# Hybrid decoder step: the S5 half turn's transfers issued by GpSimd instead of ScalarE

## What is computed

```
bb_t = coef * (B u_t)                    complex
h_t  = a * h_(t-1) + bb_t                a = exp((lam_re + i lam_im) dt)
y_t  = Re-part of C h_t + d * u_t
```

## Time and profile before

| | |
|---|---|
| median of 3 runs | 1402.5 us (1401.43 to 1403.63) |
| the profiled execution | 1399.56 us |
| its span (first to last instruction) | 1397.8 us |
| PE busy | 1322.9 us (95%), granted clock 0.979 on average |
| DVE busy | 760.2 us (54%) |
| ACT busy | 449.5 us (32%) |
| POOL busy | 397.3 us (28%) |

### The profile page before, as it was taken

How to read it: one execution, slowest core, us unless ns; L and a number is a source line. 1 busy time by engine, 2 the same in 40 slices (tenths; PEclk the granted TensorE clock), 3 DMA queues, 4 the chain that set the end, 5 groups by cost and what they waited for, 6 DMA issues and landing times.

```text
span 1397.8 us, 32218 instructions
## 1 busy us (share of the span) xinstructions
PE 1322.9 (95%) x14024; PEld 1208.2 (86%) x14024; DVE 760.2 (54%) x1499; ACT 449.5 (32%) x809; POOL 397.3 (28%) x403
## 2 busy tenths in 40 slices
PE   5999999997999999999999999999999989899997
PEld 5898999987888988989898989988897589798885
DVE  7595744625444637173554637274453648989322
ACT  7222222221423425252432525252334521023211
POOL 7226656462031302222031212212111032254000
PEclk8999999999999999999999999999997999999999
DMA  8242433334512213122221313122116286455221
GB/s 231 84 110 77 121 86 95 87 101 116 157 60 66 83 44 96 59 73 66 78 72 45 94 60 95 59 55 67 53 56 221 49 258 196 133 180 177 97 85 38
DMA packets 167725, 139.07 MB, mean 99 GB/s; under 512 B 34143, under 2 KB 156688, under 8 KB 167456
## 3 DMA queue, kind: packets, MB, share of 16 engines
q1 hardware_dynamic: 157314, 119.69, 28.9%
q10 hardware_dynamic: 10270, 17.32, 4.1%
HBM read 91.36 MB, written 42.34 MB: 96 GB/s over the span
## 4 chain that ended last, share of the span: by engine, by line
PE 54%; DVE 9%; ACT 6%; issue 3%; DMA 1%; ACTq 1%; POOL 0%; SPq 0%; DVEq 0%
PE f_ps L363 11%; PE f_ps L365 9%; PE f_ps L364 9%; PE q L2245 9%; PE q L365 2%; PE q L364 2%; PE q L363 2%; DVE early L1971 2%; PE f_ps L2135 2%; PE q L2276 2%; ACT L1383 1%; DVE up_gu L1969 1%; PE q L2262 1%; DVE w_z L1797 1%; DMA f_out<-projected 1%
## 5 line engine op out<-in xcount | busy, mean ns | idle before, releaser
L363 PE MATMUL f_ps<-h_hi,fw_hi 128*128 128x384 f32 (+1 forms) x968 | 340.6, 352 | 14.1 <-ACTq L1371 5.6
L365 PE MATMUL f_ps<-h_hi,fw_lo 128*128 128x384 f32 (+1 forms) x968 | 317.3, 328 | 0.0
L1311 POOL TENSOR_TENSOR fw_lo<-fw,fw_hi 128x1024 fp32r<-128x1024 f32 x46 | 110.2, 2395 | 651.0 <-ACT fw_hi L1369 651.0
L364 PE MATMUL f_ps<-h_lo,fw_hi 128*128 128x384 f32 (+1 forms) x864 | 282.3, 327 | 0.0
L363 PEld LDWEIGHTS f_ps<-h_hi,fw_hi 128*128 128x128 f32 x968 | 182.6, 189 | 31.3 <-issue 10.0
L365 PEld LDWEIGHTS f_ps<-h_hi,fw_lo 128*128 128x128 f32 x968 | 182.9, 189 | 0.0
L364 PEld LDWEIGHTS f_ps<-h_lo,fw_hi 128*128 128x128 f32 x864 | 163.1, 189 | 3.9 <-issue 3.8
L1383 ACT ACTIVATE f_out<-f_ps 128x384 f32<-128x384 f32 (+1 forms) x108 | 51.1, 474 | 248.9 <-PE f_ps L365 248.4
L1787 DVE TENSOR_TENSOR t_m<-t_m,q 128x256 f32<-128x256 f32 (+1 forms) x66 | 27.6, 418 | 174.2 <-PE q L2245 174.2
L363 PE MATMUL proj_ps<-h_hi,fw_hi 128*128 128x384 f32 (+1 forms) x336 | 114.5, 341 | 4.8 <-ACT proj_out L943 3.7
L364 PE MATMUL proj_ps<-h_lo,fw_hi 128*128 128x384 f32 (+1 forms) x336 | 111.2, 331 | 0.0
(11 more groups left out here) (443 smaller groups left out, 2893.8 us busy)
## 6 DMA issues: line engine op xcount, KB each, us to landing
fw<-in_w_in_dram SPq DMA_DIRECT2D x50, 512.0 KB, 4.4
projected<-f_out SPq DMA_DIRECT2D x72, 192.0 KB, 2.0
f_out<-projected SPq DMA_DIRECT2D x48, 192.0 KB, 2.5
projected<-proj_out SPq DMA_DIRECT2D x16, 544.5 KB, 3.4
raw<-projected SPq DMA_DIRECT2D x8, 838.5 KB, 6.5
projected<-f_out SPq DMA_DIRECT2D x36, 160.0 KB, 1.8
branch_z<-projected ACTq DMA_DIRECT2D x8, 544.0 KB, 5.8
xt<-in_x_prompt_dram SPq DMA_DIRECT2D x8, 512.0 KB, 5.6
```

The source lines that it names most:

```text
L363: pe.matmul(out, whi, xhi, start=first, stop=False)
L364: pe.matmul(out, whi, xlo, start=False, stop=False)
L365: return pe.matmul(out, wlo, xhi, start=False, stop=last)
L1311: pool.tensor_tensor(wlo[:, g % 2], wst[:, g % 2], whi[:, g % 2].bitcast(F32), ALU.subtract).then_inc(fw_lo, 1)
```

## The change

The two issues per third are taken out of ScalarE's list and put into GpSimd's `rotate_back`, behind the waits that stand there already and ahead of the multiplication at line 725. Source, destination, size, semaphore and count stay the same. ScalarE loses its two waits (scan, hdone) along with the issues.

```diff
@@ rotate_back on GpSimd
                         pool.wait_ge(scan, GB * b + gr.stop)
                         if at >= 2:
                             pool.wait_ge(hdone, at - 1)
+                        for to, of in ((slice(0, HD), slice(HD, P)), (slice(HD, P), slice(0, HD))):
+                            pool.dma_start(half_turn[to, at % 2, 0:n * JP].rearrange("p (g j) -> p g j", g=n), gsc[of, gr, :]).then_inc(swapped[at % 2], 16)
                         pool.tensor_tensor(t_a[:, 1 + at % 2, 0:n, :], gsc[:, gr, :], rot[:, 0, gr, :], ALU.mult).then_inc(back, 1)
@@ on ScalarE
-                def swap(b, k):
-                    gr, n, at = sub(b, k)
-                    act.wait_ge(scan, GB * b + gr.stop)
-                    if at >= 2:
-                        act.wait_ge(hdone, at - 1)
-                    for to, of in ((slice(0, HD), slice(HD, P)), (slice(HD, P), slice(0, HD))):
-                        act.dma_start(half_turn[to, at % 2, 0:n * JP].rearrange("p (g j) -> p g j", g=n), gsc[of, gr, :]).then_inc(swapped[at % 2], 16)
-
@@ s5 on ScalarE
-                    if at in (8, 9, 10):
-                        swap(b, at - 8)
```

## The result

The changed kernel takes 1405.5 us (median of 14 runs), the kernel before 1400.57 us (median of 14 runs by now, among them the three shown above). The ratio is 1.0028, with a 95% interval of 1.0015 to 1.0040: 3.9 us slower, 2.1 to 5.6 by the interval.

The account below looks back on a forecast made before the run. TensorE was taken to bound the kernel, waiting 3.9 us at line 895. Later first thirds (+1.7 us) less two vanished waits (-0.8) gave +0.9 us on the median of 1402.5: 1403.4 us, range 1400.0 to 1410.5.

Parts of the forecast that it names:

- The bound and the place: TensorE bounds, busy 1322.9 of 1397.8 us; the change acts only through its waits at line 895, 3.9 us together.
- the two short waits of 0.28 and 0.54 us: TensorE's waits at line 895 that vanish as the second third's rotation back ends earlier: -0.8 us.
- The issue's cost: Each transfer issue on GpSimd, ahead of line 725: taken as 1.0 us, between 0.57 and 2.4.
- rival of a dear issue: First pair of each batch on GpSimd: issues of 1.8 to 2.4 us give 1409.8 to about 1420; chance 0.24.
- the dear first transfer: GpSimd's first transfer, in batch 0, is dear once: up to 5 us extra, 1408.4; chance 0.07.
- the one of the ports: First pair held until VectorE's scans end, 1.5 to 2.2 us late per batch: 1409.4 to 1412; chance 0.11.
- The first third's hprev: Rotation back starts at t0 + 4.0, TensorE at t0 + 5.5; late by 0.57, 0.04, 0.17, 0.91: +1.7 us.
- the cheap issue: GpSimd issues in 0.57 us, landing 1.5 us later: -1.3 us, 1401.2; chance 0.12.
- The landing: First third's half turn lands 2.0 us after the second issue's end; VectorE then waits about 2 us per batch.
- Last third, ScalarE's 13.7 us, the next table: Last third's later hprev, ScalarE's 24 removed issues and GpSimd's delayed next table: all costed at nothing.
- The clock: Idle TensorE might be throttled at its waits; the 3.06 us stall kept 2.4 GHz, added stalls are shorter: no price.
- The sum: TensorE's waits at line 895: +1.7 us for first thirds, -0.8 for vanished short waits, +0.9 us in all.

Follow-up runs that it names:

- e9: Kernel before, unchanged, profiled and timed again; ratio 1.0002 (0.9989 to 1.0014) to the kernel before.
- e4: Kernel before, ScalarE still issuing, but holding the first third's transfers back until GpSimd has finished its correction; 0.9996 times the kernel before.
- e11: Changed kernel with 18 unused products in TensorE's last-batch wait for the first hprev; 1.0022 times the kernel before.
- e1: Changed kernel, but the first third's transfers stay on ScalarE; 0.9986 times the kernel before (0.9969 to 1.0002).
- e5: Changed kernel with the first third's two issues and multiplication moved ahead of GpSimd's correction of the weight block; 0.9963 times the kernel before.
- e3: Changed kernel, but GpSimd multiplies first and issues the two transfers behind it; 1.0043 times the kernel before.
- e8: Changed kernel with 34 unused products in TensorE's last-batch wait for the first hprev; 1.0035 times the kernel before.
- e12: The kernel of e5 once more, on another chip; 0.9983 times the kernel before (0.9968 to 0.9997).
- e10: Kernel before with 12 unused products in TensorE's last-batch wait for the first hprev; 0.9982 times the kernel before.

## Why the prediction was right or wrong

**The bound and the place**: right. All that changed on TensorE by the change itself is at line 895 (897 now), and the two short waits of 0.28 and 0.54 us vanished as forecast. That they stood there before was partly chance: e9, the same kernel, has neither.

**The issue's cost**: wrong, too dear. 1.0 us was taken between 0.57 and 2.4; it is 0.54 (24 issues). (Its upper bound was misread: the earlier trace rows have a GpSimd instruction of 2.72 us, longer than the 2.4.) The rival of a dear issue is refuted, and so are the dear first transfer (0.69 us at most) and, in its strong form, the one of the ports: the issues took 0.52 to 0.69 us with VectorE's tensor_tensor and scans beside them, and in batch 1 the first pair landed 2.1 and 2.6 us after the start of each issue while VectorE was busy throughout. The Trainium skill's inference (SBUF — State Buffer, Who interferes with whom) that tensor_tensor spares the descriptors agrees with these rows.

**The first third's hprev**: this is the step that failed, and an error in the other direction, on the issue, hid a part of it. The prediction took 0.6 us for line 793 and 0.67 from there to the end of hprev, 1.27 in all, as if the rotation back ran alone. It took 2.16, 2.66, 2.68 and 2.67 us: the second multiplication, pushed behind its own two issues, stands beside it (1.50 for line 795 in batch 0, 1.53 to 1.57 for line 798 in the others). It had not run alone before the change either, where it took 2.14 us (142.57 to 144.71). The start of line 795, forecast at 3.95 us from the correction's end (t0 + 4.0), came at 4.30 in batch 0 and 3.18 to 3.23 in the others, the cheap issue's doing. Forecast from the correction's end to hprev: 5.3 us; measured: 5.85 to 6.46. The scans, "now without line 725 beside them" in the prediction, did have it beside them (2.52 us), since it began only 1.2 us later; but they ended ahead of the landing all the same, as forecast. The rows that showed the exclusion were read and quoted; they weren't laid over the new timetable of each multiplication. By the cheap issue alone the sum would have been -1.3 us, which is further off.

Against the kernel before both theories have a part: the first third's rotation back starts 1.0 to 2.1 us later (the landing) and takes up to 0.6 us longer (the collision). Yet with ScalarE issuing at the same moment (e4) almost nothing was lost: there the second multiplication, with no issues ahead of it, ran partly in VectorE's wait. How the loss divides between the two is not shown further than that.

**The landing**: 2.0 us after the issue's end was about right in batches 1 to 3 (line 795 starts 2.2 us behind it), and 1.2 too little in batch 0 (3.2), where the second transfer landed 3.6 us after the start of its issue; why is open. A wait of VectorE of about 2 us in each batch, the sign that the prediction named, did not come (1.32, 0.25, 0.21 and 0.22).

**Last third, ScalarE's 13.7 us, the next table**: hidden, as forecast.

**The clock**: "no price" was wrong as a statement on this kernel, since one profile of it was taken for all, and "the added stalls are shorter" overlooked that the 0.91 us of batch 3 would lengthen the 3.06 already there. As a statement on the change it comes out right: e9 to e11.

**The sum**: +1.7 - 0.8 was forecast for TensorE's waits; +4.4 - 0.8 = +3.6 us came, 0.26% of the time, and 0.28% (0.15 to 0.40) was measured. The mis-sized term is the lateness of the four first thirds: 0.57, 0.04, 0.17 and 0.91 forecast, 1.65, 0.58, 0.54 and 1.64 measured. That the range held owes more to its width, made for the rivals, than to the mechanism. And 1403.4 lies as near to 1405.5 as it does by luck: it stands on a median of three executions, 1402.5, which 14 have brought down to 1400.57.

## What to carry to other kernels

Where two engines exclude each other, a small delay of one moves its instructions onto other instructions of the other: draw the new timetable of both, instruction by instruction, before costing the waits, since the same 1.1 us ahead of the second multiplication made hprev later in one timetable (the change) and 0.86 us earlier in another (e1). Look for a place where the engine waits for something else; here the first third's work cost nothing there and took nothing from VectorE (e5). And read a second profile of the same kernel before a clock that stays up in one is called safe.

## What was not expected of the hardware

A VectorE instruction was held not only by the multiplication that ran beside it but by one that had yet to start. In batch 1 of the changed kernel line 798 starts at 206.64, 0.61 us after the start of the first issue and during the second, and stands until 208.14, while the multiplication is recorded from 207.12 on; in batches 2 and 3 it starts 0.57 us after it and goes the same way. In e3 line 798 starts 0.50 us after the first issue and is held by the correction, recorded 0.59 us later. In batch 3 of e8:

```profile
329.10 1.07 POOL L726 DMA_DIRECT2D s_half_turn<-s_scan  x2 [1.22 <-DVE s_scan L815]
330.18 1.02 POOL L727 TENSOR_TENSOR s_ta<-s_scan,s_rot 128x384 f32<-128x384 f32 x1
...
329.49 0.16 DVE L798 TENSOR_TENSOR s_fin<-s_ta,s_tb 128x3 f32<-128x3 f32 x1
329.57 0.55 DVE L799 TENSOR_TENSOR s_hprev<-s_ta,s_tb 128x381 f32<-128x381 f32 x1
```

Lines 798 and 799 begin 0.39 and 0.47 us after the first issue, ahead of the second, and aren't held; hprev is done before the multiplication starts, 4.29 us after the correction instead of 5.85. Batch 2 of e8 and of e11 went the same way (line 799 0.47 and 0.48 us after the first issue). So the instruction behind the issues seems to take hold while they are still being carried out; why is open, and no run was made for it. It also means that the changed kernel's waits differ between its own executions: hprev of batch 2 is at 5.88 us in one and at 4.29 in another.

Also not expected: a wait of TensorE of about 3 us (3.06 and 3.12) is followed by the halved clock in one execution of the same kernel and not in another, at a price of 1.9 us; a wait of 2.33 us (e1) was followed by it too, and one of 1.54 us (e5, e12) was not. With the wait filled by unused products (e8, e10, e11) the clock stayed up in all three profiles.
